# Diagonals made on ScalarE, slot weights ahead of the flips, memory's roots taken once, and a later overflow table in a two-layer decoder trunk

## The reference, cut to what matters

```
for l in range(DEPTH):
    h = rms_norm(x, norm_mix[l])
    ...
    m = rms_norm(mem, norm_mem[l])          # only the gain norm_mem[l] changes
    x = x + cross_attention(h, m, ...)
    h = rms_norm(x, norm_ffn[l])
    x = x + hier_moe(h, w_group[l], ..., w_gate[l], w_up[l], w_down[l])

def hier_moe(...):                          # top-1 group, then top-2 experts in it
    ...
    return (jax.nn.silu(xb @ w_gate[e]) * (xb @ w_up[e])) @ w_down[e]   # times the token's weight
```

## Time and profile before

| | before |
|---|---|
| median of 3 runs | 1143.96 us |
| lowest and highest | 1142.73 and 1144.92 us |
| the profiled execution's own time | 1144.17 us |
| its span | 1142.4 us |
| mean granted TensorE clock | 0.98 |
| PE, DVE, ACT, POOL busy | 1093.0, 667.6, 366.2, 104.8 us |

### The profile page before, as it was taken

How to read it: one execution, slowest core, us unless ns; L and a number is a source line. 1 busy time by engine, 2 the same in 40 slices (tenths; PEclk the granted TensorE clock), 3 DMA queues, 4 the chain that set the end, 5 groups by cost and what they waited for, 6 DMA issues and landing times.

```text
span 1142.4 us, 18266 instructions
## 1 busy us (share of the span) xinstructions
PE 1093.0 (96%) x5644; PEld 569.2 (50%) x5644; DVE 667.6 (58%) x1572; ACT 366.2 (32%) x811; POOL 104.8 (9%) x177
## 2 busy tenths in 40 slices
PE   7999999999799999999989999999996999999996
PEld 4854555556563333333457545555465633333333
DVE  4336765467683555555652477655776745555555
ACT  5226331114433333333152163311243433333331
POOL 1000000000048100000000000000002470000001
PEclk9999999999888999999999999999997999999999
DMA  9031024500338999999640300245005389999992
GB/s 353 1 103 45 1 74 147 221 1 1 135 122 349 429 427 429 429 428 429 255 157 26 122 1 1 74 147 221 1 1 221 142 371 431 426 428 431 426 428 79
DMA packets 37103, 243.22 MB, mean 213 GB/s; under 512 B 4976, under 2 KB 15248, under 8 KB 23984
## 3 DMA queue, kind: packets, MB, share of 16 engines
q1 hardware_dynamic: 36224, 240.77, 52.1%
q0 software_dynamic: 384, 1.31, 0.3%
q10 hardware_dynamic: 432, 0.38, 0.1%
HBM read 240.36 MB, written 2.10 MB: 212 GB/s over the span
## 4 chain that ended last, share of the span: by engine, by line
PE 81%; DVE 11%; issue 2%; ACT 2%; DVEq 1%; DMA 1%; ACTq 0%; SPq 0%; POOLq 0%; POOL 0%
PE ps L2888 19%; PE ps L2419 12%; PE ps L2912 9%; PE ps L2684 9%; PE ps L2847 8%; PE ps L2409 7%; PE ps L2387 5%; PE ps L2732 2%; PE ps L2502 2%; PE ps L2446 2%; DMA X<-in_x 1%; PE ps L2542 1%; DVE xgT L2142 1%; DVE xlo L2125 1%; PE ps L2452 1%
## 5 line engine op out<-in xcount | busy, mean ns | idle before, releaser
L2888 PE MATMUL ps<-wgu,xw 128*64 128x512 f32 x1024 | 230.3, 603 | 0.5 <-ACTq L1412 0.5
L2232 DVE TENSOR_TENSOR X<-ps,X 128x512 f32<-128x512 f32 x245 | 152.1, 683 | 16.7 <-PE ps L2847 10.5
L2419 PE MATMUL ps<-hT,ring 128*128 128x512 f32 x352 | 156.8, 595 | 0.0
L2888 PEld LDWEIGHTS ps<-wgu,xw 128*64 128x64 f32 x1024 | 71.5, 138 | 135.3 <-issue 130.3
L2912 PE MATMUL ps<-wdn,hhT 128*32 128x512 f32 x1024 | 116.5, 595 | 0.0
L2684 PE MATMUL ps<-ring,yT 128*128 128x512 f32 x256 | 115.3, 597 | 1.0 <-DVE ssqY L1909 0.8
L2419 PEld LDWEIGHTS ps<-hT,ring 128*128 128x128 f32 x352 | 64.6, 190 | 69.8 <-issue 69.8
L2847 PE MATMUL ps<-yhi,Wt 64*128 64x512 f32 x384 | 84.1, 425 | 2.2 <-DVEq L1521 2.1
L1072 ACT ACTIVATE xw<-xgT 128x512 f32 (+1 forms) x132 | 75.2, 616 | 22.0 <-issue 11.5
L2237 DVE TENSOR_TENSOR hh<-ps,silu 128x256 f32<-128x256 f32 x32 | 13.6, 424 | 116.3 <-ACTq L1440 115.9
L2245 DVE SCALAR_TENSOR_TENSOR ylo<-ps,ws,yhi 128x512 fp32r<-128x512 f32 x64 | 48.0, 751 | 54.9 <-ACTq L1458 54.1
(11 more groups left out here) (388 smaller groups left out, 1387.9 us busy)
## 6 DMA issues: line engine op xcount, KB each, us to landing
wgu<-in_w_gate_up SPq DMA_DIRECT2D x64, 2048.0 KB, 14.9
wdn<-in_w_down_pairs SPq DMA_DIRECT2D x32, 2048.0 KB, 16.1
ring<-in_w_in SPq DMA_DIRECT2D x8, 1024.0 KB, 6.6
ring<-in_w_mix_out SPq DMA_DIRECT2D x12, 512.0 KB, 6.3
w_kv<-in_xa_w_kv SPq DMA_DIRECT2D x4, 1024.0 KB, 8.7
ring<-in_w_in SPq DMA_DIRECT2D x2, 2048.0 KB, 15.4
ring<-in_w_in SPq DMA_DIRECT2D x2, 1536.0 KB, 13.8
memx<-in_mem SPq DMA_DIRECT2D x4, 512.0 KB, 3.8
```

Source lines behind the costliest of these rows:

```text
L2232: tt(xh, bank, xh, ALU.add).then_inc(mfreed((what, n)), 1)
L2419: last = mm(bank, w[:, c, c0:c0 + P], hT[:, c, :], start=c == 0, stop=c == KD - 1)
L2888: last = mm(bank[r], xw[:, c, j, 0:SLOTS], wgu[parity][:, 2 * c // KD, j, c % (KD // 2)], start=c == 0, stop=c == KD - 1)
```

## The change

Four edits. (1) The eight diagonals are made by ACT, one copy with a scale for each, ahead of `gated(0, True)`; DVE's function `placed` keeps two small operations and signals `srel_ready`, and ACT signals `place_ready`. (2) On PE `slot_weights()` now stands ahead of `hidden_turned(0)`. (3) Memory's squares and roots are taken in layer 0 alone. (4) POOL starts the overflow table only when `hh` of pair 3 is there, and PE reads the overflow count behind the last `bring_back` instead of ahead of the last two.

```
                 wait_apart(pool, S["params_free"], l + 2)
+                wait_apart(pool, S["hh_ready"], mdone(l, 3, "hh_ready", 1))
                 overflow_table()
...
                 act.wait_ge(S["layer_done"], l + 1)
-                for i in range(NM):
-                    act.wait_ge(mem_in[i], (l + 1) * 16)
-                    square(xn[:, i], memx[:, i], accum_out=mem_s[:, 0, i:i + 1])
-                    act.drain()
-                act.nop().then_inc(S["mem_ssq"], 1)
+                if l == 0:
+                    for i in range(NM):
+                        act.wait_ge(mem_in[i], 16)
+                        square(xn[:, i], memx[:, i], accum_out=mem_s[:, 0, i:i + 1])
+                        act.drain()
+                    act.nop().then_inc(S["mem_ssq"], 1)
...
                 first_windows(slice(KD // 2, KD), "xw_ready")
+                act.wait_ge(S["srel_ready"], done(l, "srel_ready", 1))
+                for k in range(2):
+                    for t in range(NT):
+                        copy(diag[:, k * NT + t], ident[:], scale=srel[:, k, t:t + 1])
+                act.drain()
+                act.nop().then_inc(S["place_ready"], 1)
                 gated(0, True)
...
-                dve.wait_ge(S["mem_ssq"], done(l, "mem_ssq", 1))
-                mean_eps(stat[:, 0:NM], mem_s[:, 0], D)
-                rsqrt(mem_s[:, 1], stat[:, 0:NM], NM)
-                signal("mem_rstd")
+                if l == 0:
+                    dve.wait_ge(S["mem_ssq"], 1)
+                    mean_eps(stat[:, 0:NM], mem_s[:, 0], D)
+                    rsqrt(mem_s[:, 1], stat[:, 0:NM], NM)
+                    signal("mem_rstd")
...
                 def placed():
-                    shape = [P, 2 * NT, P]
-                    tt(diag[:], ident[:].unsqueeze(1).to_broadcast(shape),
-                       flat(srel).unsqueeze(2).to_broadcast(shape), ALU.mult)
                     ts(all_ones[:], iota[:, 0:P], 0.0, 1.0, ALU.mult, ALU.add)
                     nc.vector.tensor_copy(slot[:], slot_0[:])
-                    signal("place_ready")
+                    signal("srel_ready")
...
                 gate_up(0, 0, 0)
                 slot_places()
+                slot_weights()
                 hidden_turned(0)
-                slot_weights()
                 gate_up(1, 1, 0)
...
                 bring_back(PAIRS - 2, "last comb", 1, 0, closes=False)
-                wait_apart(pe, S["route_ready"], l + 2)
-                n_ovf = pe.value_load(ovf[0:1, 0:1], min_val=0, max_val=OVF - 1)
-                before = pe.value_load(ovf[0:1, 1:2], min_val=0, max_val=DEPTH * OVF)
...
                 bring_back(PAIRS - 1, "last comb", 1, 1, opens=False)
+                wait_apart(pe, S["route_ready"], l + 2)
+                n_ovf = pe.value_load(ovf[0:1, 0:1], min_val=0, max_val=OVF - 1)
+                before = pe.value_load(ovf[0:1, 1:2], min_val=0, max_val=DEPTH * OVF)
```

More of the change, by code:

```diff
@@ L418 @@
     max_ready=14, p_ready=14, pn_ready=14, x1_updated=NT, x2_updated=NT, G_ready=NT, G_used=2,
-    xgT_act=KD, xgT_dve=KD, xw_half=1, spans_ready=1, kept_open=2, ranks_kept=1, later_chosen=1, params_free=1, place_ready=1, ranked_ready=1, places_ready=2, ws_ready=1, rank_read=1, rank_kept=1,
+    xgT_act=KD, xgT_dve=KD, xw_half=1, spans_ready=1, kept_open=2, srel_ready=1, ranks_kept=1, later_chosen=1, params_free=1, place_ready=1, ranked_ready=1, places_ready=2, ws_ready=1, rank_read=1, rank_kept=1,
     qx_ready=NT, qx_squared=NT, xq_ssq=NT, qx_reduced=NT, qxT_ready=NT, oTx_ready=NT, lg_ready=NT,
@@ L1168, in _ @@
                 normalise(l, 1)
-                act.wait_ge(S["mem_rstd"], done(l, "mem_rstd", 1))
+                act.wait_ge(S["mem_rstd"], 1)
                 for i in range(NM):
```

## The result

The changed kernel takes 1147.34 us (median of 15 runs, 1145.63 to 1148.5), against 1144.1 us before on the same chip (15 runs, 1141.31 to 1148.0). The ratio is 1.0022, 95% interval 1.0012 to 1.0032, or about +2.5 us (+1.4 to +3.7); the two medians themselves lie 3.2 us apart. The forecast was 1144.8 us.

The account below looks back on a forecast made before the run. PE bounds the kernel, busy 1093.0 of 1142.4 us. Heads +0.4 and +1.85, boundary -0.6, end -0.9 sum to +0.75 on 1144.17, an execution 0.21 above the median: 1144.8 us forecast, whole range 1141.5 to 1147.6.

Parts of the forecast that it names:

- no change: Whole kernel: a measured time between 1141.7 us (below is faster, 0.14) and 1146.25 us (above is slower, 0.23).
- The head's order: Each layer's head: gate_up(1) waits for ACT's xw, not the slot weights; +0.4 us in layer 0, +1.85 in layer 1.
- The term of the eight copies: ACT in each head: eight scaled diagonal copies take 2.17 us, bounds 1.23 and 3.1.
- The clock: PE in both heads: the fall to 0.50 and its loss on gate_up(1) stay the same, 0; bounds -1.8 to +1.8.
- the thin stretch: PE between gate_up(0) and gate_up(1): 6.4 and 6.6 us after the change, where it was 6.0 and 4.8.
- the four terms' sum: Two heads, layers' boundary and program's end: forecast +0.4 + 1.85 - 0.6 - 0.9 = +0.75 us.
- The rival of the lower clock: Heads: clock stays low longer, +0.9 us in each layer, no gain at the boundary; 1147.2 us, chance 0.22.
- The boundary: Between the layers: PE's moved reads end pair 15's idle but precede the memx flips; -0.6 us, bounds -1.1 and +0.3.
- code-fetch rival: Layers' boundary: the branch waits for its code, +0.3 us instead of -0.6; 1145.7 us, no chance of its own given.
- The end: Program's end: the gap ahead of pair 15's bring_back goes with the moved reads; -0.9 us, bounds -0.5 and -0.94.
- The roots: Layers' boundary: memory's squares (some 2.5 us) and root operations lie beside PE's L2542, so dropping them brings 0.
- The table: POOL's overflow table moves from the head to beside steps 4 to 6; it costs nothing in either place.

Follow-up runs that it names:

- e5: Changed kernel with a Silu of one unused column behind ACT's copy of the ranks, so Silu's table loads earlier; 1143.74 us, ratio 0.9991.
- e6: Changed kernel with ACT's six register reads for pair 1 ahead of its wait for srel and the eight copies; 1144.92 us, ratio 0.9999.
- e12: Changed kernel with three unused matmuls on PE, two behind the slot weights and one behind the flips of hh; 1142.65 us, ratio 0.9976.
- e2: Kernel before with one edit: PE reads the overflow count behind the last bring_back; 1145.35 us, ratio 1.0001.
- e3: Kernel before with one edit: memory's squares and roots in layer 0 alone; 1145.87 us, ratio 1.0003.
- e4: Changed kernel with POOL's overflow table back in the head, its new wait taken out; 1147.31 us, ratio 1.0025.
- e10: Kernel before with one edit: slot_weights ahead of hidden_turned(0) on PE; 1140.61 us, ratio 0.9965.
- e1: Changed kernel with the diagonals made by DVE in one operation again, DVE signalling place_ready; 1138.93 us, ratio 0.9944.
- e9: Changed kernel with the diagonals made by POOL in one operation in place of ACT's eight copies; 1139.51 us, ratio 0.9947.

## Why the prediction had the order right and came out 2.5 us low

The measured 1147.34 us lies inside the stated range, 0.26 us below its upper edge. It lies outside the 1143.0 to 1146.4 us that the forecast itself covered, and above the 1146.25 us from which the prediction counts as slower, a case to which it gave 0.23. So the case that it held likeliest, no change, is not what came.

**The head's order: right.** ACT's `xw` became the last to arrive. The table load came at 345.89; counted from `srel`'s end that is 6.15 us, where the prediction had 5.95 (338.25 to 344.2). The start of `gate_up(1)` moved by +0.70 us in layer 0 (forecast +0.4) and +1.81 us in layer 1 (+1.85). The term of the eight copies was a little low: 2.45 and 2.44 us, against 2.17 taken from the `hmT` copies. The estimate of 2.4 us by the formula of the Trainium skill, page "ScalarE: Activation LUTs", section "What ACT_TABLE_LOAD costs", was nearer, and this trace agrees with it. e5 and e6 show that reads, copies and table stand one behind the other.

**The clock: the mis-sized term.** The prediction put 0 because the thin stretch was not shorter. Measured by the profiled executions it is -0.28 us in layer 0 and +1.10 in layer 1, together +0.82, which is over half of the 1.29 us between the four terms' sum (+2.04) and the forecast's +0.75. The rest is layer 0's start (+0.3) and the boundary (+0.24), less small amounts at the end and at layer 1's start. The error was to reason from how long the thin stretch is. What counted was how long the low stretch lasts and how much of it lies on `gate_up(1)`: in after it was about 6.8 us in both layers, begun 3.6 us ahead of `gate_up(1)` in layer 0 and 1.2 us ahead in layer 1. e12 shows that the fall in after needs PE's waits, for with them filled there is none. Why it lasts 3.4 us in one head and 6.8 in another, and why it begins where it does, no run shows.

The prediction's argument against a longer low stretch was that `gate_up(1)` lost the same in both layers of before, 1.8 and 1.7 us. That was a coincidence: the stretch was 6.8 us long in layer 0, with half of it on the slot weights (3.13 us there, 1.87 in layer 1), and 3.4 us in layer 1, all of it on `gate_up(1)`. The rival of the lower clock, with +0.9 in each layer, came true in one. That its figure, 1147.2, is the measured one within 0.2 us is luck: it also had no gain at the boundary, where 0.36 us came.

**The base: one execution.** Layer 1's head was 20.61 us in the profile of before. In the five other heads with unchanged code (before's layer 0, e2, e3) it was 21.90 to 22.19. The low stretch was short there, about 3.4 us, and about 6.8 us in the others. Unedited, the kernel takes anything from 1141 to 1149 us. Its time goes with its mean granted clock: of the 86 runs of before beside the experiments, the 18 with a clock of 0.984 or 0.985 took 1141.1 to 1144.5 us, the 12 with 0.979 or less 1144.8 to 1148.8. After's 15 runs have 0.978 to 0.983. Against the usual head the change's terms sum to about +0.6, against the profiled one to +2.04; the ratio says +2.5 (+1.4 to +3.7). A mean over a whole execution does not tell which head was low, so how often the short stretch comes is not known, and the difference between these sums stays open.

**The boundary: right sign, -0.36 against -0.6.** PE stands 1.56 us ahead of the flips where I had 1.17 + 0.15; whether the reads or the branch take the 0.24 us more is not shown. The +0.3 of the code-fetch rival did not come. **The end: right,** -0.93 in after and -0.91 in e2 against -0.9. **The roots: right,** 0 by e3. **The table: right,** 0 by e4.

**What the prediction did not see.** It took the four edits as one sum near zero, and costed the swap only in the order of after, where ACT hides it. By itself the swap is a gain of about 4 us (e10): `slot_weights` fills the wait for `hh`, and the flips then stand directly ahead of `gate_up(1)`, so that it starts 2.0 and 0.6 us sooner than in before, in layer 1 with none of it at the lower clock. Edit 1 takes 8 us away (e1). With the moved reads, -1.3, the sum is near what was measured: a small number made of two large ones. The rows for it were there: PE's 3.13 us of slot weights on the chain, and `silu` done 1.3 us ahead of `hh`.

## What to carry to other kernels

Before work is moved to an engine with spare time, read what stands behind the place where it is put: here 2.45 us of copies pushed 3.3 us of register reads, a table load and a gather, none of it on the chain before, on to the path. Cost edits apart as well as together, since a good reordering can hide inside a bundle that is slower. Where PE idles just ahead of dense work, ask what the clock does there: a useless 128x512 matmul that fits inside the wait may be worth more than it costs, and one that does not fit is paid in full.

## What the runs showed that was not expected

- The same small matmuls on PE went with a fall of the clock in one kernel and not in another: after had `slot_weights` (16 of 128x32, 1.97 us), two flips and waits of 1.9 and 1.5 us in the head and fell to 0.50; with three 128x512 fillers more (2.98 us in all) it stayed at 1.00 in both layers. It also stayed up without any filler in layer 1 of e1, e9 and e10, with one wait of 0.9 to 1.4 us, though not in layer 0 of the same three.
- The low stretches in the heads were of two lengths, about 3.4 us (before's and e6's layer 1, layer 0 of e1, e9 and e10) and about 6.8 us (layer 0 of before and e6, both layers of after, e2, e3, e4 and e5).
- A DVE operation on 128x4 beside POOL's 2.09 us product took 1.13 instead of 0.16 us.
- Six register reads cost ACT 3.27 to 3.30 us wherever they stood (3.55 once, in layer 1 of before), some 0.55 us each.
